# Up projections of a two-part transformer kernel: gate and value columns interleaved in the weight pieces, so that each stationary tile is every second column

## The chip, the cores and the metric

The kernel runs on one core of one Trainium2 chip. The time is device microseconds of one execution. The kernel before took 2694.57 us, the median of 3 runs (2691.31, 2694.57 and 2696.43 us).

## The reference, cut to what matters

The input is one sequence of 512 tokens with 1024 features in float32. A first block (an indexer-sparse attention beside a latent attention) is followed by four layers, each with a mixer (differential, stick-breaking, sliding-window, differential) and a feed-forward part; a norm closes it. The change touches the feed-forward part of the four layers alone. What that part computes is, as its kernel uses it:

```python
g = rmsnorm(h, ffn_norm) @ w_up          # w_up is 1024 x 5504: 2752 gate columns, then 2752 value columns
g = causal_conv_width_3(g) + conv_b      # per column
hidden = silu(g[:, :2752]) * g[:, 2752:]
h = h + hidden @ w_down
```

Every gate column is multiplied with the value column of the same number, so a gate tile and its value tile of 128 columns are produced one after the other.

## The kernel before, in words

Activations lie transposed: features on the 128 partitions, the 512 tokens along the free dimension, so 1024 features are KT = 8 tiles. Weights come from the host as "pieces" of 128 x 2048 floats (1 MB), cut and ordered there (`weight_pieces`, `piece`). Three slots of SBUF hold three pieces. SP loads a piece into `raw` when the piece three before it has been used (L1252). ACT copies it to `whi` in the reduced-precision form of float32 (L1270), and GpSimd writes `wlo` = `raw` - `whi` in four parts over the same memory (L1219). The activations are split in the same way into `xh` and `xl`.

A product of full precision is then three matmuls, issued by `three_passes` (L481): `whi` x `xh`, `whi` x `xl`, `wlo` x `xh`, all into one PSUM bank. In a feature piece the weights are the stationary operand (128 x 128) and the activations the moving one (128 x 512). A matmul record comes with a weight-load record (LDWEIGHTS); in the rows "ring<-xh,wlo" is a matmul with `wlo` stationary and `xh` moving.

An up stage (`up`, L1134) handles 22 pieces. Each of the first 21 holds, for every k of the 8 feature tiles, 256 columns: 128 gate columns, then the 128 value columns that belong to them. `first_piece` (piece 0, in an order of its own because its activations are only just being split, with the norm's sum of squares between) and `feature_piece` (pieces 1 to 20) both call `feature_group(slot, half, k, ...)`, which takes columns k*256 + half*128 to k*256 + half*128 + 127: half 0 is the gate, half 1 the value. That is 21 x 2 x 8 x 3 = 1008 passes a layer, 4032 in the kernel. Piece 21 holds only 64 gate and 64 value columns side by side; it is one stationary tile of 128 contiguous columns and 24 passes a layer.

The results go round four PSUM banks (`ring`). VectorE multiplies each with the norm's factor (L2405, into `u`), ScalarE makes the first tap of the convolution (L1695) and the silu (L1698), VectorE the other taps (L2391), the product (L2415), and the split of the hidden activations for the down projection (L2417, L2419). The engines run through fixed programs and meet at counting semaphores; each queue is in the order that the Python loops issue. `feature_group` is also called by `index_q`, by the latent stages, by `project` and by `early_out`, for pieces whose layout is not touched.

Of the kernel before, what the change touches and what calls it, by code (L numbers as in the profile page):

```python
# [14 lines left out]
P = 128  # L15
S = 512
D = 1024
KT = D // P
# [456 lines left out]
def three_passes(pe, out, w_hi, w_lo, x_hi, x_lo, first, last, weights_stationary=True):  # L475

    passes = [(w_hi, x_hi), (w_hi, x_lo), (w_lo, x_hi)]
    if not weights_stationary:
        passes = [(x_hi, w_hi), (x_hi, w_lo), (x_lo, w_hi)]
    for n, (stationary, moving) in enumerate(passes):  # L480
        ins = pe.matmul(out, stationary, moving, start=first and n == 0, stop=last and n == 2)  # L481
    return ins


def tensor_program(pe, m, st, plan):
    by_vector = vector_pieces(st)

    def wait_piece(b, k):

        p = b.at("piece", k)  # L490
        if p in by_vector:
            pe.wait_ge(m["own_lo"], by_vector.index(p) + 1)
        else:
            pe.wait_ge(m["lo_done"], p - sum(v < p for v in by_vector))

    def wait_unit_free(b, k):

        if b.at("unit_taken", k) >= 4:
            pe.wait_ge(m["unit_taken"], b.at("unit_taken", k) - 3)

    def feature_group(slot, half, k, x, out):

        w = slice(k * 256 + half * P, k * 256 + (half + 1) * P)
        return three_passes(pe, out, m.whi[slot][:, w], m.wlo[slot][:, w], *x, k == 0, k == KT - 1)

    def first_piece(b, nb, signal):


        wait_piece(b, 0)
        slot = b.slot("piece", 0, SLOTS)  # L510
        out = [m.ring[b.slot("unit_ready", half, 4)][:] for half in range(2)]
        for half in range(2):
            wait_unit_free(b, half)
            for k in range(KT - 1):
                if half == 0:
                    pe.wait_ge(m["xl_ready"], b.at("xl_ready", k + 1 - KT))
                feature_group(slot, half, k, X[k], out[half])
                yield
        pe.wait_ge(m["xl_ready"], b.at("xl_ready", 0))
        for half in range(2):  # L520
            feature_group(slot, half, KT - 1, X[KT - 1], out[half]).then_inc(m[signal], 1)
            if half == 0:
                square_sum(nb)
            yield

    def feature_piece(b, j, xs):

        wait_piece(b, j)
        slot = b.slot("piece", j, SLOTS)
        for half in range(2):  # L530
            wait_unit_free(b, 2 * j + half)
            out = m.ring[b.slot("unit_ready", 2 * j + half, 4)][:]
            for k in range(KT):
                ins = feature_group(slot, half, k, xs[k], out)
            ins.then_inc(m["unit_ready"], 1)

    def token_group(slot, t, k, out):
# [18 lines left out]
    X = [(m.xh[:, k, :], m.xl[:, k, :]) for k in range(KT)]  # L556

    def square_sum(nb):

        pe.wait_ge(m["sq_added"], nb.at("sq_added", 0))  # L560
        pe.matmul(m.out[:], m.ones[:], m.var[:], start=True, stop=True).then_inc(m["sq_summed"], 1)
# [570 lines left out]
        work.finish()  # L1132

    def up(b, nb):  # L1134
        for _ in first_piece(b, nb, "unit_ready"):
            pass
        for j in range(1, LAST):
            feature_piece(b, j, X)
        wait_piece(b, LAST)
        slot, unit = b.slot("piece", LAST, SLOTS), 2 * LAST  # L1140
        wait_unit_free(b, unit + 1)
        for k in range(KT):
            w = slice(k * P, (k + 1) * P)
            ins = three_passes(pe, m.ring[b.slot("unit_ready", unit, 4)][:], m.whi[slot][:, w], m.wlo[slot][:, w],
                               *X[k], k == 0, k == KT - 1)
        ins.then_inc(m["unit_ready"], 2)

    for name in plan:
        b = st[name]
# [1380 lines left out]
def piece(w):  # L2530

    k, n = w.shape
    kt = -(-k // P)
    a = np.zeros((kt * P, n), w.dtype)
    a[:k] = w
    a = a.reshape(kt, P, n).transpose(1, 0, 2).reshape(P, kt * n)
    if kt * n == 2048:
        return a
    full = np.zeros((P, 2048), w.dtype)
    full[:, :kt * n] = a  # L2540
    return full


def column_pieces(w):
    return [piece(w[:, c:c + 256]) for c in range(0, w.shape[1], 256)]


def mixer_pieces(mixer, w):
    if mixer == "window":
        q, k, v = (column_pieces(part) for part in np.split(w, [D, D + 256], axis=1))  # L2550
        return [k[0], q[0], v[0], *q[1:]]
    q, k, v = np.split(w, 3, axis=1)
    out = []
    for t in range(TILES):
        out.append(piece(np.concatenate([q[:, P * t:P * t + P], k[:, P * t:P * t + P]], axis=1)))
        if t % 2:
            out += column_pieces(v[:, 256 * (t // 2):256 * (t // 2) + 256])
    return out


def weight_pieces(x):
    w = x["w_in"][0]
    q_a, k_a, v_a, g_a, q_i, k_i, w_i, c_q, c_kv, k_r, g_b = np.split(
        w, np.cumsum([512, 512, 512, 512, 512, 64, 8, Q_LORA, KV_LORA, B_ROPE]), axis=1)
    rest = np.concatenate([c_q[:, 256:], k_i, w_i, k_r, np.zeros((D, 24), w.dtype)], axis=1)
    out = []
    for part in (rest, q_i, c_q[:, :256]):
        out += column_pieces(part)
    out += [piece(x["w_uq"][0][:, c:c + 384]) for c in (0, 384)]
    out += column_pieces(c_kv)  # L2570
    out.append(piece(x["w_ukv"][0]))
    for part in (k_a, q_a, v_a):
        out += [piece(part[:512]), piece(part[512:])]
    for part in (g_b, g_a):
        out += column_pieces(part)
    out += column_pieces(np.concatenate([x["w_out"][0][512:], x["w_out"][0][:512]]))
    for l in range(N_LAYERS):
        name = {"diff": "da", "stick": "sb", "window": "sw"}[MIXER[l]]
        out += mixer_pieces(MIXER[l], x[f"{name}_w_qkv_2"][MIXER[:l].count(MIXER[l])])
        out += column_pieces(x["w_o_2"][l])  # L2580
        up, f = x["ffn_w_up_2"][l], x["ffn_w_up_2"].shape[2] // 2
        for t in range(F_TILES):
            n = min(P, f - t * P)
            out.append(piece(np.concatenate([up[:, t * P:t * P + n], up[:, f + t * P:f + t * P + n]], axis=1)))
        down = x["ffn_w_down_2"][l]
        for c in range(0, D, 256):
            k = 0
            for nk in DOWN_K:
                rows = np.zeros((nk * P, 256), w.dtype)
                got = down[k * P:(k + nk) * P, c:c + 256]  # L2590
                rows[:got.shape[0]] = got
                if got.shape[0] < nk * P:
                    rows[-HALF:] = got[-HALF:]
                out.append(piece(rows))
                k += nk
    return np.stack(out)
# [73 lines left out]
```

## Time and profile before

| what | value |
|---|---|
| median of 3 runs | 2694.57 us (2691.31 to 2696.43) |
| span of the profiled execution | 2693.6 us |
| TensorE matmul records | 2653.5 us busy (99%), 12935 |
| TensorE weight-load records | 2126.5 us busy (79%), 12935 |
| VectorE, ScalarE, GpSimd busy | 1460.7, 1122.8, 1167.0 us (54, 42, 43%) |
| mean granted TensorE clock | 0.997 |
| DMA | 253.44 MB, mean 94 GB/s |

The profiled execution is given by its span, from the first to the last instruction; what lies around the span (launch and end) has no row. The span is 1.0 us under the median and 2.8 us under the highest of the runs. How to read the rows: PE is TensorE's matmuls, PEld its weight loads, which run beside them; DVE is VectorE, ACT ScalarE, POOL GpSimd, SP the queue that issues most DMAs. Matmul records overlap one another, since they contain the time through the array, so that the distance from one start to the next tells the pace and the length of a record does not.

### The profile page before, as it was taken

The page shows a single profiled execution, that of the slowest core. Times are in us where ns is not written, and L with a number is a line of the kernel's source. Part 1 is how long each engine was busy: PE and PEld are TensorE (multiplying, and loading weights), DVE is VectorE, ACT ScalarE, POOL GpSimd, SP SyncE. Part 2 cuts the span into 40 slices and gives each one's busy share as a digit, 9 for nine tenths or more (in the row PEclk, how much of TensorE's full clock was granted, in tenths as well). Part 3 has the DMA queues.
Part 4 walks back from the last instruction along what each step waited for, and adds up shares of the span by engine and source line. Part 5 has one row for each costly group of instructions (what it writes and reads, how often), then busy time and mean ns, then how long its engine had stood idle before and what let it go on. Part 6 is the DMA issues. An engine that isn't in the chain of part 4 may idle for free.

```text
span 2693.6 us, 32187 instructions
## 1 busy us (share of the span) xinstructions
PE 2653.5 (99%) x12935; PEld 2126.5 (79%) x12935; DVE 1460.7 (54%) x2615; ACT 1122.8 (42%) x1521; POOL 1167.0 (43%) x880
## 2 busy tenths in 40 slices
PE   8999999999999999999999999999999999999998
PEld 7787677778888877778888876888888777888887
DVE  5888556657554145657554145575522565575522
ACT  4544544444333236653333236443333344443332
POOL 3454443335445532335445541354455332454453
PEclk9999999999999999999999999999999999999999
DMA  4224032222223221112223331222233222222232
GB/s 164 79 94 172 1 133 86 70 73 96 106 96 110 104 88 63 63 65 98 104 94 110 109 110 48 79 94 98 106 109 110 94 87 71 94 94 94 94 122 81
DMA packets 46597, 253.44 MB, mean 94 GB/s; under 512 B 4528, under 2 KB 11200, under 8 KB 18928
## 3 DMA queue, kind: packets, MB, share of 16 engines
q1 hardware_dynamic: 35376, 231.92, 24.3%
q10 hardware_dynamic: 11072, 19.47, 2.2%
q8 instruction: 102, 1.67, 0.2%
q14 instruction: 47, 0.39, 0.0%
HBM read 249.21 MB, written 10.55 MB: 96 GB/s over the span
## 4 chain that ended last, share of the span: by engine, by line
PE 92%; DVE 4%; ACT 2%; POOL 1%; issue 1%; DMA 0%; SPq 0%; DVEq 0%; ACTq 0%
PE ring L481 79%; PE ring L978 3%; PE turn L983 2%; PE turn L481 1%; PE out L1022 1%; POOL wlo L1219 1%; PE ring L776 1%; PE ring L645 1%; PE out L792 1%; DVE sp L2238 1%; PE out L1028 0%; DVE e L2206 0%; PE out L1110 0%; ACT whi L1270 0%; DVE z L2241 0%
## 5 line engine op out<-in xcount | busy, mean ns | idle before, releaser
L1219 POOL TENSOR_TENSOR wlo<-raw,whi 128x512 fp32r<-128x512 f32 x840 | 1121.8, 1367 | 1456.9 <-ACT whi L1270 1456.8
L481 PE MATMUL ring<-xh,whi 128*128 128x512 f32 x1888 | 753.4, 399 | 9.3 <-DVE xl L1753 8.4
L481 PE MATMUL ring<-xh,wlo 128*128 128x512 f32 x1888 | 736.6, 390 | 0.0
L481 PE MATMUL ring<-xl,whi 128*128 128x512 f32 x1888 | 736.5, 390 | 0.0
L1270 ACT ACTIVATE whi<-raw 128x2048 fp32r<-128x2048 f32 x215 | 411.3, 1914 | 437.1 <-DMA raw<-in_pieces 421.8
L481 PEld LDWEIGHTS ring<-xh,whi 128*128 128x128 f32 x1888 | 354.9, 188 | 114.9 <-issue 41.1
L481 PEld LDWEIGHTS ring<-xh,wlo 128*128 128x128 f32 x1888 | 354.9, 188 | 75.3
L481 PEld LDWEIGHTS ring<-xl,whi 128*128 128x128 f32 x1888 | 355.2, 188 | 72.3 <-issue 3.4
L2391 DVE SCALAR_TENSOR_TENSOR taps<-u,conv,taps 128x511 f32<-128x511 f32 (+1 forms) x344 | 295.7, 905 | 17.3 <-ACT taps L1695 14.8
L2405 DVE TENSOR_TENSOR u<-ring,r 128x512 f32<-128x512 f32 x168 | 114.4, 687 | 299.7 <-PE ring L481 299.7
L481 PE MATMUL ring<-hh,whi 128*128 128x512 f32 (+1 forms) x693 | 265.3, 383 | 0.0
L481 PE MATMUL ring<-hl,whi 128*128 128x512 f32 (+1 forms) x693 | 265.1, 383 | 0.0
L481 PE MATMUL ring<-hh,wlo 128*128 128x512 f32 (+1 forms) x693 | 265.1, 383 | 0.0
L1695 ACT ACTIVATE taps<-u,conv 128x512 f32<-128x512 f32 x172 | 137.9, 809 | 304.5 <-DVE u L2405 304.5
L2379 DVE TENSOR_TENSOR h<-ring,h 128x512 f32<-128x512 f32 x64 | 44.1, 689 | 317.8 <-PE ring L861 277.2
L481 PE MATMUL ring<-whi,xh 128*128 128x256 f32 (+1 forms) x576 | 180.9, 314 | 0.8 <-POOL wlo L1219 0.8
L481 PE MATMUL ring<-wlo,xh 128*128 128x256 f32 (+1 forms) x576 | 172.9, 300 | 0.0
L481 PE MATMUL ring<-whi,xl 128*128 128x256 f32 (+1 forms) x576 | 172.8, 300 | 0.0
L481 PEld LDWEIGHTS ring<-hh,wlo 128*128 128x128 f32 x693 | 130.2, 188 | 25.5
L481 PEld LDWEIGHTS ring<-hh,whi 128*128 128x128 f32 x693 | 130.2, 188 | 25.4
L481 PEld LDWEIGHTS ring<-hl,whi 128*128 128x128 f32 x693 | 130.2, 188 | 25.4
L1698 ACT ACTIVATE taps<-taps 128x512 f32<-128x512 f32 x88 | 55.7, 633 | 172.3 <-DVE taps L2391 172.3
(304 smaller groups left out, 3423.0 us busy)
## 6 DMA issues: line engine op xcount, KB each, us to landing
raw<-in_pieces SPq DMA_DIRECT2D x215, 1024.0 KB, 4.8
toep<-diag_store ACTq DMA_DIRECT2D x16, 512.0 KB, 3.6
diag_store<-diag_row ACTq DMA_DIRECT2D x1, 5120.0 KB, 25.6
band_store<-band_row ACTq DMA_DIRECT2D x1, 3072.0 KB, 33.1
h<-in_x SPq DMA_DIRECT2D x4, 512.0 KB, 6.3
wbias<-band_store ACTq DMA_DIRECT2D x4, 512.0 KB, 7.2
raw<-in_pieces SPq DMA_DIRECT2D x4, 256.0 KB, 6.4
result<-h SPq DMA_DIRECT2D x2, 512.0 KB, 3.0
```

The costliest lines, as they stand in the source:

```text
L481: ins = pe.matmul(out, stationary, moving, start=first and n == 0, stop=last and n == 2)
L645: ins = pe.matmul(out, x[:, tok], weights[slot][:, w], start=begins, stop=ends)
L776: pe.matmul(bank(("score", p, j, i))[:, 0:n], q[:, i * P:(i + 1) * P], k[:, 0:n], start=True, stop=True).then_inc(m["unit_ready"], 1)
L978: pe.matmul(m.ring[2 + j][:, 0:n], qs[part, i * P:(i + 1) * P], ks[part, lo:lo + n], start=True, stop=True).then_inc(m["su_ready"], 1)
L983: ins = pe.transpose(m.turn[:, to:to + P], src[:, at:at + P], m.ident[:])
L1219: ins = pool.tensor_tensor(m.wlo[slot][:, part], m.raw[slot][:, part], m.whi[slot][:, part].bitcast(F32), ALU.subtract)
L1270: act.activation(m.whi[p % SLOTS][:], m.raw[p % SLOTS][:], ACT.Copy).then_inc(m["hi_done"], 1)
L1695: act.activation(taps[g][:], m.u[g][:], ACT.Identity, scale=cols[:, 4 * g + 2:4 * g + 3], bias=cols[:, 4 * g + 3:4 * g + 4]).then_inc(m["t ...
L1698: act.activation(taps[0][0:rows, :], taps[0][0:rows, :], ACT.Silu).then_inc(m["silu"], 1)
L2379: dve.tensor_tensor(m.h[:, k, :], ring(b, k)[:], m.h[:, k, :], ALU.add).then_inc(m["unit_taken"], 1)
L2391: dve.scalar_tensor_tensor(y[:, shift:S], m.u[g][:, 0:S - shift], cols[:, tap:tap + 1], y[:, shift:S], ALU.mult, ALU.add).then_inc(m[signa ...
L2405: dve.tensor_tensor(m.u[g][:], ring(b, 2 * t + g)[:], m.r[:], ALU.mult).then_inc(m["unit_taken"], 1)
```

## The change

In pieces 0 to 20 of every up stage the host lays gate and value columns alternately: gate 0, value 0, gate 1, value 1 and so on, 256 columns for each k as before. `feature_group` gets a flag `paired`; with it the stationary tile is every second column of the 256, from column `half` on, 128 columns at a distance of 8 bytes, where it was 128 adjacent columns at a distance of 4 bytes. `first_piece` and `feature_piece` pass the flag on, and only `up` sets it. Piece 21 keeps its layout and its code.

```diff
-    def feature_group(slot, half, k, x, out):
+    def feature_group(slot, half, k, x, out, paired=False):
 
         w = slice(k * 256 + half * P, k * 256 + (half + 1) * P)
+        if paired:
+            w = slice(k * 256 + half, (k + 1) * 256, 2)
         return three_passes(pe, out, m.whi[slot][:, w], m.wlo[slot][:, w], *x, k == 0, k == KT - 1)
...
     def up(b, nb):
-        for _ in first_piece(b, nb, "unit_ready"):
+        for _ in first_piece(b, nb, "unit_ready", True):
             pass
         for j in range(1, LAST):
-            feature_piece(b, j, X)
+            feature_piece(b, j, X, True)
...
         for t in range(F_TILES):
             n = min(P, f - t * P)
-            out.append(piece(np.concatenate([up[:, t * P:t * P + n], up[:, f + t * P:f + t * P + n]], axis=1)))
+            pair = [up[:, t * P:t * P + n], up[:, f + t * P:f + t * P + n]]
+            out.append(piece(np.stack(pair, axis=2).reshape(D, 2 * n) if n == P else np.concatenate(pair, axis=1)))
```

## Rows read from the trace of the kernel before

**Rows 1.** The page: span, busy shares, TensorE clock, shares of the last-ending chain.
```profile
span 2693.6 us, 32187 instructions
...
PE 2653.5 (99%) x12935; PEld 2126.5 (79%) x12935; DVE 1460.7 (54%) x2615; ACT 1122.8 (42%) x1521; POOL 1167.0 (43%) x880
...
PEclk9999999999999999999999999999999999999999
...
PE 92%; DVE 4%; ACT 2%; POOL 1%; issue 1%; DMA 0%; SPq 0%; DVEq 0%; ACTq 0%
```

**Rows 2.** Chain in order of time, layer 2: start us, length us, what.
```profile
1746.02 6.40 POOL wlo L1219 x4
1752.42 0.04 issue
1752.47 237.61 PE ring L481 x1047
```

**Rows 3.** Four up stages by windows: busy us (and count) of each engine.
```profile
core 0: us, PE busy (x) PEld busy (x) DVE busy (x) ACT busy (x) POOL busy (x), PEclk, DMA share, GB/s
605.60:860.00 254.40, 254.18 (x1119) 209.77 (x1119) 150.97 (x227) 97.43 (x95) 123.79 (x95) 1.00 0.28 100
1210.90:1465.30 254.40, 254.17 (x1120) 209.78 (x1119) 152.01 (x227) 97.63 (x95) 123.42 (x95) 1.00 0.28 100
1730.00:1984.00 254.00, 253.78 (x1118) 209.46 (x1117) 154.85 (x227) 97.71 (x95) 126.09 (x97) 1.00 0.28 100
2329.00:2583.00 254.00, 253.79 (x1118) 209.47 (x1117) 152.35 (x228) 97.63 (x95) 123.93 (x95) 1.00 0.28 100
```

**Rows 4.** Timeline inside an up stage, matmuls and weight loads: start us, length us.
```profile
640.15 0.39 PE L481 MATMUL ring<-xh,whi 128*128 128x512 f32 x1
640.16 0.19 PEld L481 LDWEIGHTS ring<-xl,whi 128*128 128x128 f32 x1
640.38 0.39 PE L481 MATMUL ring<-xl,whi 128*128 128x512 f32 x1
640.38 0.19 PEld L481 LDWEIGHTS ring<-xh,wlo 128*128 128x128 f32 x1
```

**Rows 5.** Timeline around the only wait of TensorE in an up stage.
```profile
627.78 0.19 PEld L481 LDWEIGHTS ring<-xh,whi 128*128 128x128 f32 x1 [0.64 <-POOL wlo L1219]
627.78 0.50 PE L481 MATMUL ring<-xh,whi 128*128 128x512 f32 x1 [0.22 <-POOL wlo L1219]
627.89 0.19 PEld L481 LDWEIGHTS ring<-xl,whi 128*128 128x128 f32 x1
628.12 0.40 PE L481 MATMUL ring<-xl,whi 128*128 128x512 f32 x1
628.12 0.19 PEld L481 LDWEIGHTS ring<-xh,wlo 128*128 128x128 f32 x1
```

**Rows 6.** Timeline of a value projection of layer 0, whose moving operand has 256 columns.
```profile
540.19 0.28 PE L481 MATMUL ring<-whi,xl 128*128 128x256 f32 x1
540.31 0.28 PE L481 MATMUL ring<-whi,xh 128*128 128x256 f32 x1
...
540.19 0.19 PEld L481 LDWEIGHTS ring<-whi,xh 128*128 128x128 f32 x1
540.31 0.19 PEld L481 LDWEIGHTS ring<-wlo,xh 128*128 128x128 f32 x1
```

**Rows 7.** Groups of weight loads, whole span: busy us, mean ns of one, idle before.
```profile
L481 PEld LDWEIGHTS ring<-xh,wlo 128*128 128x128 f32 x1888 | 354.9, 188 | 75.3
L1022 PEld LDWEIGHTS out<-aT,v 128*128 128x128 f32 x128 | 23.8, 189 | 19.0 <-issue 13.1
L1110 PEld LDWEIGHTS out<-at_w,v_w 128*64 128x64 f32 x224 | 12.1, 137 | 2.9 <-issue 2.9
```

**Rows 8.** Waits inside an up stage, 628 to 860 us: total, times, longest us.
```profile
POOL wlo L1219 <- ACT whi L1270: 115.6, 23, 6.1
ACT taps L1695 <- DVE u L2405: 77.3, 23, 4.3
DVE u L2405 <- PE ring L481: 75.8, 18, 4.6
ACT taps L1698 <- DVE taps L2391: 38.6, 21, 4.2
ACT whi L1270 <- DMA raw<-in_pieces: 25.1, 18, 7.1
DVE taps L2391 <- ACT taps L1695: 3.7, 13, 1.1
PE ring L481 <- POOL wlo L1219: 0.2, 1, 0.2
```

**Rows 9.** The page: DMA issues of the weight pieces, and ACT's and GpSimd's work on them.
```profile
L1219 POOL TENSOR_TENSOR wlo<-raw,whi 128x512 fp32r<-128x512 f32 x840 | 1121.8, 1367 | 1456.9 <-ACT whi L1270 1456.8
L1270 ACT ACTIVATE whi<-raw 128x2048 fp32r<-128x2048 f32 x215 | 411.3, 1914 | 437.1 <-DMA raw<-in_pieces 421.8
...
raw<-in_pieces SPq DMA_DIRECT2D x215, 1024.0 KB, 4.8
```

More of the change, by code:

```diff
@@ L499, in wait_unit_free, with first_piece @@
             pe.wait_ge(m["unit_taken"], b.at("unit_taken", k) - 3)
-    def feature_group(slot, half, k, x, out):
+    def feature_group(slot, half, k, x, out, paired=False):
         w = slice(k * 256 + half * P, k * 256 + (half + 1) * P)
+        if paired:
+            w = slice(k * 256 + half, (k + 1) * 256, 2)
         return three_passes(pe, out, m.whi[slot][:, w], m.wlo[slot][:, w], *x, k == 0, k == KT - 1)
-    def first_piece(b, nb, signal):
+    def first_piece(b, nb, signal, paired=False):
         wait_piece(b, 0)
@@ L516, in first_piece @@
                     pe.wait_ge(m["xl_ready"], b.at("xl_ready", k + 1 - KT))
-                feature_group(slot, half, k, X[k], out[half])
+                feature_group(slot, half, k, X[k], out[half], paired)
                 yield
@@ L520, in first_piece @@
         for half in range(2):
-            feature_group(slot, half, KT - 1, X[KT - 1], out[half]).then_inc(m[signal], 1)
+            feature_group(slot, half, KT - 1, X[KT - 1], out[half], paired).then_inc(m[signal], 1)
             if half == 0:
@@ L524, in first_piece, with feature_piece @@
             yield
-    def feature_piece(b, j, xs):
+    def feature_piece(b, j, xs, paired=False):
         wait_piece(b, j)
@@ L533, in feature_piece @@
             for k in range(KT):
-                ins = feature_group(slot, half, k, xs[k], out)
+                ins = feature_group(slot, half, k, xs[k], out, paired)
             ins.then_inc(m["unit_ready"], 1)
```

## Prediction, made before the changed kernel ran

> **What bounds the kernel now.** I read the page first: TensorE's matmul records cover 99% of the span, the chain that ended last is TensorE for 92% of it, and the granted clock stands at its top digit, that is 2.4 GHz, in all 40 slices [rows 1]. Then the chain in order of time, to see what it consists of where the change acts. In layer 2 one unbroken run of 1047 passes of the helper at L481 takes 237.61 us, so one pass every 237.61/1047 = 226.9 ns; the same figure for the same count stands in the chain of the other three layers [rows 2]. The windows then show each up stage as nothing but TensorE: about 254 of 254 us, while VectorE has 151 to 155 us of work, ScalarE 98 and GpSimd 123 to 126 [rows 3]. The waits say the same from the other side: VectorE, ScalarE and GpSimd wait for what comes before them, and TensorE waits once, for 0.2 us, for GpSimd's low half of piece 2 [rows 5, 8]. So inside an up stage the time is a count of passes times the distance between their starts. The question is only whether that distance stays at 226.9 ns.
>
> The timeline shows what makes up the distance. Each weight load starts when the matmul before its own starts (640.16 beside 640.15, 640.38 beside 640.38) and its record is 0.19 us, so it ends before the next matmul begins [rows 4]. The load is thus covered by the previous matmul, and what matters is how long it really occupies its path. The record is longer than that. After the one wait, the load at 627.78 is followed by the next load at 627.89, and its own matmul, whose record is 0.50 instead of 0.39 us, is late by the same 0.11 us [rows 5]. Where the moving operand has only 256 columns, loads with records of 0.19 us start every 0.12 us and overlap one another [rows 6]. A load of 128 columns occupies the path for about 0.11 us, then, and has 0.2269 us to do it: a good half of the pass is spare.
>
> **The change part by part.**
>
> *Strided weight loads.* 4 layers x 21 pieces x 2 halves x 8 tiles x 3 passes = 4032 loads now step over 8 bytes from column to column instead of 4. Their number, columns, partitions and bytes used are as before. No row of the trace shows a load with a step, so its price has to be bounded. Every nanosecond that it adds to the distance between passes costs 4032 ns = 4.03 us. The lower bound on the cost is zero with the load's pace unchanged: the mean length of a load goes by its columns, 137 ns for 64 and 189 for 128, 0.81 ns a column [rows 7]. The next bound is a load whose pace goes by the stretch of memory it walks, 1024 bytes instead of 512: 2 x 0.11 = 0.22 us, under 0.2269, so still hidden; taken at the coarse end of the rounding, 0.23 us, it would stick out by 3.1 ns, 4032 x 3.1 ns = 12.5 us. The upper bound is a load that is no more covered at all and adds its 0.11 us to every pass, as after the wait [rows 5]: 4032 x 0.11 = 444 us. For a gain the bound is the part of a pass that isn't streaming: 256 more moving columns take 226.9 - 120 = 107 ns [rows 2, 6], so 512 take 214 and 13 ns are left; if the load made them and a step removed them, 4032 x 13 ns = 52 us would go. I see no reason why a step should.
>
> I take zero. The row it is nearest to is TensorE's other read: the moving operand walks 512 x 4 = 2048 bytes a partition in each 226.9 ns, 9.0 bytes a ns, at full pace [rows 2, 4]. A stepped load walks 1024 bytes, and if it spread them over the pass it would need only 4.5 bytes a ns; at the old 0.11 us it needs 9.3, which is what the other read does already.
>
> A rule of the Trainium skill stands against this. "Advanced Engine Details and Errata", section Memory Cachelines, says that SBUF is read in lines of 16 bytes, that accesses that stay in a line run at full pace while a different line at each access is penalised, and that two hits on a line are needed to absorb the latency; for PSUM, whose lines it gives as 8 bytes, it says that any non-contiguous pattern slows matmuls significantly. By its SBUF half a step of 8 bytes still hits each line twice and the sum stays at zero; by its PSUM half, if the load followed it, the load would double and be the second bound above. No row of the trace before tells the two apart.
>
> *The first load after a pause.* There the load is not covered [rows 5]. That happens once at the wait of each layer; if the load doubled, each would cost 0.11 us, 4 x 0.11 = 0.4 us in all. At an unchanged pace it is nothing. No other load in the stage is first after a pause.
>
> *The pieces and their path.* The host reorders columns inside a piece. The DMA still moves 1024 KB in one issue for each of the 215 pieces, ScalarE's copy is still 128 x 2048 in 1914 ns and GpSimd's four subtractions still 128 x 512 in 1367 ns [rows 9]: they read and write the whole piece in order. Cost nothing, with no cover needed. The stationary tile holds the same numbers in the same columns, so PSUM, the norm factor, the convolution's coefficients and the rest of VectorE's and ScalarE's work see the same operands. Piece 21, the mixers and the down stages use contiguous columns as before. No wait, no issue and no semaphore is added or moved, and no queue is passed.
>
> *Sum.* 2693.6 + 0 = 2693.6 us of span. The median of the runs is 1.0 us above this span; I give 2694.6 us. A measurement of this kernel can tell about 0.2% from no change, that is 5.4 us; the cost at which the change would be seen is therefore 1.3 ns a pass.
>
> **The rivals.**
>
> *The load doubles but stays in its cover.* For it: more memory is walked for each load. Against: the pace of the moving read. The load records would grow from 188 by the 104 ns that 128 columns at 0.81 take, to about 292 ns, and the distance would be 227 to 230 ns: 2694.6 to 2707 us. Chance 0.10, of which 0.06 on the side that cannot be measured.
>
> *The load outlasts the matmul (slower).* Place: the load path of the 4032 passes. It decides from an occupation of 226.9 ns on, 2.06 times the present 0.11; from there the distance is the load's own. At three times it is 0.33 us: (330 - 226.9) x 4032 = 416 us, 3110 us. The same comes out of a stepped load that isn't taken ahead of the running matmul (444 us, 3139 us). For it: the load would be the only operand of TensorE in this kernel that is not read contiguously, and nothing in the trace shows that path with a step. Against: it would need more than the doubling that the memory walked can explain. Chance 0.08.
>
> *A shorter pass (faster).* 52 us at most, 2642 us. Nothing speaks for it but the bound. Chance 0.02.
>
> *The change doesn't do what it says.* A load of a stepped tile could be issued as several loads. Then the count of weight loads would leave 12935; its time would go by whether the pieces fit the 0.2269 us, so it shares the two cases above rather than having a price of its own.
>
> **How the numbers follow.** The forecast, no visible change, has 0.80. Its own range is the spread of the runs, 2691 to 2696, widened to 2687 to 2701 for another set of three. The doubled load reaches to 2707. Together these hold 0.90; I set the range to 2687 to 2709 and leave out the load that outlasts the matmul and the shorter pass. Within 0.2%: 0.80 + 0.06, less 0.01 for a forecast case that measures off, 0.85. Slower: 0.04 + 0.08 = 0.12. Faster: 0.02 + 0.01 = 0.03.
>
> **What the profile of the changed kernel would show.** If the step is free: weight loads in `ring<-xh,wlo` still at 188 ns, 12935 of them, the chain's run of 1047 passes still 237.6 us. If the load doubled under cover: a minimum near 188 and a maximum near 292 ns in that group, matmuls still 0.227 us apart, and the first matmul after the wait at piece 2 late by 0.22 instead of 0.11 us. If the load binds: the run of passes in the up stages longer than 237.6 us with everything else as it was, VectorE waiting longer for `ring`, and TensorE's 0.2 us wait for GpSimd gone. I would be wrong if a pass in an up stage stands more than 1.3 ns further from the next than before.

## The result, and the profile after

The changed kernel took 2720.24 us (median of 4 runs, 2718.94 to 2721.48) against 2695.5 us for the kernel before: a ratio of 1.0095, 95% interval 1.0082 to 1.0107. The 2695.5 us are the median of 4 runs, one of which took 9223.89 us; that one is not in the ratio, and the other three have a median of 2694.57 us. The changed kernel is slower by 25 us, where no change was forecast, and outside the range of 2687 to 2709. In the profiled executions the span went from 2693.6 to 2718.9 us, 25.3 us more.

The page of the kernel after, against [rows 1]:

```profile
span 2718.9 us, 32187 instructions
...
PE 2680.5 (99%) x12935; PEld 2149.0 (79%) x12935; DVE 1449.9 (53%) x2615; ACT 1122.3 (41%) x1521; POOL 1163.9 (43%) x880
```

The counts of instructions are those of before, so no load was split into several. VectorE, ScalarE and GpSimd have the same counts, and nearly the same busy times, as before. TensorE's matmul records grew by 27 us in sum, its loads by 22.5 us. The chain in order of time of the kernel after, layer 0:

```profile
599.99 15.49 PE ring L481 x67
615.47 0.86 PE out L563 x2
616.33 255.47 PE ring L481 x1098
```

Nothing but TensorE is in it any more. Before, the chain went through ScalarE's copy and GpSimd's 6.40 us [rows 2] up to the wait at piece 2; both have dropped out of it, since TensorE comes to piece 2 later. What is left of the wait is short:

```profile
628.13 0.20 PEld L481 LDWEIGHTS ring<-xh,whi 128*128 128x128 f32 x1 [0.35 <-POOL wlo L1221]
628.13 0.51 PE L481 MATMUL ring<-xh,whi 128*128 128x512 f32 x1
628.25 0.20 PEld L481 LDWEIGHTS ring<-xl,whi 128*128 128x128 f32 x1
```

The first load still waits 0.35 us for GpSimd where it waited 0.64 [rows 5], and no matmul is put down as waiting any more. So the loss is not a new wait. These lines show something else: the load at 628.13 has a step and is not covered, and the next load starts 0.12 us after it, where it was 0.11 [rows 5]. In the starts of the trace that is 117 ns against 108. The load with a step did not double.

The windows of the same 200 us inside the up stage of layer 0, matmuls of `three_passes` alone (length, busy us and count, granted clock as a share of 2.4 GHz, DMA share, GB/s), first of the kernel before, then of the kernel after:

```profile
640.00:840.00 200.00, 200.00 (x884) 1.00 0.28 100
```

```profile
640.00:840.00 200.00, 200.00 (x859) 1.00 0.27 95
```

The clock is full in both and TensorE is never idle, but 25 passes fewer fit in. Groups of one tile, min/median/max of a record in ns, in 40 us of that stage, before and after:

```profile
L481 PE MATMUL ring<-xl,whi x60: 389/389/389, 639.7 to 679.8; 128*128 128x512 f32 x60
L481 PEld LDWEIGHTS ring<-xh,whi x59: 187/188/188, 639.9 to 679.4; 128*128 128x128 f32 x59
```

```profile
L481 PE MATMUL ring<-xl,whi x58: 394/394/394, 639.7 to 679.6; 128*128 128x512 f32 x58
L481 PEld LDWEIGHTS ring<-xh,whi x58: 193/193/193, 639.9 to 679.8; 128*128 128x128 f32 x58
```

A load's record is 5 ns longer, a matmul's too, and not one of them is an exception, although ScalarE, GpSimd, VectorE and the DMAs start and stop their work many times in those 40 us. A loss to another engine should come and go with that engine's work. The distance from start to start, in the timeline of the kernel after over 40 passes:

```profile
649.70 0.39 PE L481 MATMUL ring<-xh,wlo 128*128 128x512 f32 x1
...
659.04 0.39 PE L481 MATMUL ring<-xh,whi 128*128 128x512 f32 x1
```

9.34 / 40 = 233.5 ns; over a whole unit the trace gives 233.3, against 226.7 before. 4032 passes x 6.66 ns = 26.9 us. The shorter wait for GpSimd (0.3 us less in each layer, 1.2 us) comes off, and each up stage is 6.3 us longer, 25.3 us for four: the whole difference.

In all that follows "distance" is the mean distance from one matmul's start to the next within a unit of 24 passes, without its first three, read from the starts in the timeline of layer 0; "plain" is a tile of adjacent columns, "stepped" one of every second column. A "unit" is the gate or the value product of one piece, and a piece has one of each.

### The profile page after: what moved, and what is told of

Same layout as the page of the kernel before. It is cut to its first block, busy times and chain, and to the rows that moved or that the text cites. A ratio compares the mean times of both kernels' runs of the same rounds, so it can differ in the third digit from the quotient of the medians.

```text
span 2718.9 us, 32187 instructions
## 1 busy us (share of the span) xinstructions
PE 2680.5 (99%) x12935; PEld 2149.0 (79%) x12935; DVE 1449.9 (53%) x2615; ACT 1122.3 (41%) x1521; POOL 1163.9 (43%) x880
## 4 chain that ended last, share of the span: by engine, by line
PE 95%; DVE 3%; ACT 1%; issue 1%; POOL 0%; DMA 0%; SPq 0%; DVEq 0%; ACTq 0%
PE ring L481 81%; PE ring L980 3%; PE turn L985 2%; PE turn L481 1%; PE out L1024 1%; PE ring L647 1%; PE ring L778 1%; PE out L794 1%; DVE sp L2240 1%; PE out L1030 0%; DVE e L2208 0%; PE out L1112 0%; DVE z L2243 0%; PE out L1072 0%; PE out L563 0%
## 5 line engine op out<-in xcount | busy, mean ns | idle before, releaser
L481 PEld LDWEIGHTS ring<-xh,whi 128*128 128x128 f32 x1888 | 362.1, 192 | 115.5 <-issue 41.2
L481 PEld LDWEIGHTS ring<-xh,wlo 128*128 128x128 f32 x1888 | 361.9, 192 | 76.8
L481 PEld LDWEIGHTS ring<-xl,whi 128*128 128x128 f32 x1888 | 362.3, 192 | 73.9 <-issue 3.3
L2393 DVE SCALAR_TENSOR_TENSOR taps<-u,conv,taps 128x511 f32<-128x511 f32 (+1 forms) x344 | 282.8, 866 | 24.3 <-ACT taps L1697 23.6
L481 PEld LDWEIGHTS ring<-whi,xh 128*128 128x128 f32 x576 | 110.4, 192 | 21.1 <-issue 13.9
```

The source lines that it names most:

```text
L2393: dve.scalar_tensor_tensor(y[:, shift:S], m.u[g][:, 0:S - shift], cols[:, tap:tap + 1], y[:, shift:S], ALU.mult, ALU.add).then_inc(m[signa ...
```

## The experiments

The diffs are against the changed kernel and are cut; `...` marks a cut. The host's side is cut throughout: it goes back to the layout before in `step3`, `offset1`, `offset4`, `narrow_plain`, `w384_plain`, `offsets` and `moving_step`, and is laid out to fit in `step4` and `step8`. Most of these kernels compute a product of other columns or tokens than the reference's, as their expectations say; they are for their times. From `step3` on, each ran once, beside one run of the kernel before (2693.86 to 2696.37 us).

### Whose cost is it: the step, or the new order of the data?

`host_only` keeps the host's new order and takes plain tiles. `value_only` steps in half of the loads.

```diff
# host_only
-        if paired:
-            w = slice(k * 256 + half, (k + 1) * 256, 2)
# value_only
-        if paired:
+        if paired and half == 1:
             w = slice(k * 256 + half, (k + 1) * 256, 2)
```

> The pieces keep the new order of columns from the host, but every stationary tile is again 128 adjacent columns (so a tile holds half of a gate tile and half of its value tile, and the hidden features are not the reference's). If the step of the load is the cause: the distance between passes in an up stage goes back from 233.3 to 226.7-226.9 ns and the time to 2694 to 2696 us, ratio to the kernel before 1.000. If the new order of the data is the cause (other values in the same places, the DMA or the split): it stays at 233 ns and 2720 us.

> Only the value tile (half 1) is read with the step, the gate tile (half 0) as 128 adjacent columns; the gate product is therefore of other columns than the reference's. 2016 stepped loads instead of 4032. If each stepped load costs its own matmul 6.5 ns: the 24 passes of a gate unit 226.7 ns apart, those of a value unit 233.3 ns, and half the loss, 2695.5 + 12.6 = 2708 us. If the odd start column (4 bytes off) makes the cost rather than the step: nearly the whole loss stays, 2720 us. If the stage loses for another reason (contention with the engines that write the pieces): no clean split by unit.

Measured: `host_only` 2694.62 us, ratio 0.9999 (0.9990 to 1.0009). `value_only` 2707.38 us, ratio 1.0047 (1.0032 to 1.0062), half the loss, with 226.7 ns in the gate units and 233.3 in the value units that alternate with them. The cost goes with the addressing of the unit's own loads, and it begins and ends with the unit. Data, DMA and the split are out.

### More step

`step4` and `step8` interleave two and four feature tiles in the same manner; `step3` takes every third column.

```diff
# step4: tile = every 4th of 512 columns; step8: every 8th of 1024
-            w = slice(k * 256 + half, (k + 1) * 256, 2)
+            w = slice(512 * (k // 2) + 2 * (k % 2) + half, 512 * (k // 2 + 1), 4)
...
# step3
+            w = slice(min(k, 6) * 256 + half, min(k, 6) * 256 + 384, 3)
```

> Two feature tiles are interleaved, so that a stationary tile is every fourth column (16 bytes) of 512. If the cost goes by how many different 16-byte stretches a load touches (32 adjacent, 64 with step 2, 128 with step 4): three times the extra, +20 ns a pass, 247 ns, 2695.5 + 4032 x 0.020 = 2776 us. If any step costs the same: 233.3 ns and 2720 us. If the load's pace by bytes walked decides and was hidden at step 2: 4 x 0.11 = 0.44 us a pass, 3550 us.

> Four feature tiles interleaved, every eighth column (32 bytes) of 1024. If the cost goes by 16-byte stretches touched: 128 of them as with step 4, so the same time as step4. If it goes by the memory walked: seven times the extra of step 2, +46.7 ns a pass, 273 ns, 2883 us. If any step costs the same: 2720 us.

> Every third column (12 bytes) of 384 (the last feature tile takes the one before it; the product is of other columns than the reference's). If a load keeps its pace as long as two of its columns share a 16-byte stretch on average at least, and halves it below that: 1.33 columns a stretch here, so a load record between 193 (step 2) and 310 ns (step 4), near 260, and a distance of 233 to 235 ns. If the halving comes only when every column has a stretch of its own: 193 ns. Time near 2721 to 2725 us either way.

Measured: `step4` 2725.05 us, ratio 1.0112 (1.0095 to 1.0129); `step8` 2767.3 us, 1.0269 (1.0254 to 1.0284); `step3` 2726.97 us. The distances are 235.0, 244.3 and 235.8 ns. None of the theories had that order: step 3 costs a little more than step 4, step 4 hardly more than step 2, and step 8 much more than step 4. The load records, `step3`, `step4`, `step8`:

```profile
L481 PEld LDWEIGHTS ring<-xl,whi x57: 252/252/253, 640.0 to 679.6; 128*128 128x128 f32 x57
```

```profile
L481 PEld LDWEIGHTS ring<-xh,whi x57: 308/310/311, 639.9 to 679.4; 128*128 128x128 f32 x57
```

```profile
L481 PEld LDWEIGHTS ring<-xl,whi x55: 324/331/337, 639.9 to 679.6; 128*128 128x128 f32 x55
```

Here the load really becomes slower: 188 ns with adjacent columns, 193 with step 2, 252 with step 3, 310 with step 4, and no more than 331 with step 8. How long a load really occupies its path shows at the wait at piece 2. There `step4` has

```profile
625.83 0.31 PEld L481 LDWEIGHTS ring<-xh,whi 128*128 128x128 f32 x1 [0.15 <-POOL wlo L1221]
625.84 0.62 PE L481 MATMUL ring<-xh,whi 128*128 128x512 f32 x1
...
626.04 0.33 PEld L481 LDWEIGHTS ring<-xl,whi 128*128 128x128 f32 x1
```

The next load follows after 108 ns with adjacent columns, 117 with step 2, 165 with step 3 and 211 with step 4, by the starts in the traces (`step8` has no such wait). At step 4 a load is thus twice as long, and the pass is still only 235.0 ns: the cover held. So two things are to be told apart, the load's length, which is hidden up to step 4, and a few ns a pass that are not. Whether the load of `step8` still fits its pass of 244.3 ns is open.

### Is the loss in the load's own time?

`offset1` and `offset4` use plain tiles, of the layout before, that begin one and four columns further on, all but the last value tile of a piece.

```diff
         w = slice(k * 256 + half * P, k * 256 + (half + 1) * P)
-        if paired:
-            w = slice(k * 256 + half, (k + 1) * 256, 2)
+        if paired and (k, half) != (KT - 1, 1):
+            w = slice(w.start + 1, w.stop + 1)        # offset4: 4
...
```

> Adjacent columns again, but every tile but the last begins one column (4 bytes) further on, so that its first and last 16-byte stretch are cut; the product is of shifted columns. If the 6.6 ns of step 2 come from an access that is not whole 16-byte stretches from a 16-byte boundary: 233.3 ns and 2720 us here too. If they come from the step: 226.7 ns and 2695 us.

> As offset1, with every tile but the last four columns (16 bytes) further on. If it is the cut 16-byte stretches at a tile's ends that cost offset1 its 5.8 ns a pass: none here, 226.7 ns and 2695 us. If any start other than a multiple of 512 bytes costs: 232 ns and 2714 us.

Measured: 2714.42 and 2712.61 us. There is no step in either, and most of the loss is there: 232.4 and 232.7 ns in `offset1`, 233.2 to 233.4 in three of the four layers of `offset4`. The tile's records in `offset1`, 40 us of layer 0:

```profile
L481 PE MATMUL ring<-xl,whi x58: 388/392/399, 639.8 to 679.6; 128*128 128x512 f32 x58
L481 PEld LDWEIGHTS ring<-xh,whi x58: 187/187/188, 640.1 to 679.8; 128*128 128x128 f32 x58
```

The loads are as fast as ever (187 ns, and 109 ns to the next one after the wait), and only the matmuls are late. That ends the theory that a pass loses because its load takes longer. 16-byte stretches that are cut at a tile's ends aren't it either, since `offset4`, shifted by 16 bytes, has none.

`offset4` holds another thing. Windows of 200 us in the up stages of layer 0 and layer 2, same program, same instructions:

```profile
640.00:840.00 200.00, 200.00 (x860) 1.00 0.27 94
...
1770.00:1970.00 200.00, 200.00 (x883) 1.00 0.27 95
```

From piece 3 on, layer 2 ran at 226.7 ns, the other three layers at 233.3. The same addresses have two steady rhythms. The trace shows where they part: layers 0 and 2 have the same distances, ns for ns, up to the wait before piece 2, where the distance is 332 ns in layer 0 and 327 in layer 2. After it the pattern of distances stands in another order, and at the last tile of piece 2, the one without a shift, layer 2 goes over to 226.7 ns and keeps it. The 5 ns in that wait are the first difference that the trace shows, so a small delay seems to decide the pace of the rest of the stage; no other run tests it.

### Narrower moving operands

In pieces 1 to 20, `narrow_plain` and `narrow_step` do the 512 tokens in two halves of 256, and `w384_plain` and `w384_step` compute 384 of the 512. In each pair only the loads differ.

```diff
# narrow_*
-            for k in range(KT):
-                ins = feature_group(slot, half, k, xs[k], out, paired)
+            for tok in TOKENS if paired else (slice(0, S),):
+                for k in range(KT):
+                    ins = feature_group(slot, half, k, [v[:, tok] for v in xs[k]], out[:, tok], paired)
...
# w384_*
+            n = 384 if paired else S
...
+                ins = feature_group(slot, half, k, [v[:, 0:n] for v in xs[k]], out[:, 0:n], paired)
```

> In pieces 1 to 20 of each up stage the moving operand is cut into two halves of 256 tokens, adjacent columns, pieces as before the change: 7680 passes in place of 3840. From the projections of the kernel before, 120 ns a pass: 240 instead of 226.7 ns for 512 tokens, 3840 x 13.3 = 51 us more than 2695.5, 2747 us, if GpSimd's split of the pieces keeps up (a piece needs 11.5 us of TensorE and 5.4 us of GpSimd).

> The same cut with the stepped loads of the change, against narrow_plain. If a stepped load adds a fixed time that no matmul covers: 126.7 ns a pass, 7680 x 6.67 = 51 us more than narrow_plain, plus 192 x 6.67 = 1 us for piece 0. If a stepped load really takes twice its time and was hidden: at 120 ns it isn't any more, and a pass is 213 ns or more, over 700 us more. If it only slows the moving operand's read while both run: the load runs beside the whole of a narrow pass, so again about 6.67 ns a pass.

> Pieces 1 to 20 of each up stage compute 384 of the 512 tokens, adjacent columns; the rest of a bank is left from before, so the hidden features of tokens 384 to 511 are not the reference's. Stream 160.0 ns and the 13.3 ns that every plain pass has shown beyond its stream: 173.3 ns a pass, 3840 x 53.3 = 205 us less, 2490 us.

> As w384_plain with the stepped loads. At 512 moving columns the step cost 6.67 ns a pass and at 256 nothing. If the loss is a rounding of the pass to a grid of 6.67 ns (all mean distances so far are multiples of that over a short repeating pattern): 173.3 or 180.0 ns or a pattern between. If the loss grows with the part of a pass in which no load runs: half of it, 176.7 ns. If the loss is there as soon as the load ends before the stream: 180 ns.

Measured: `narrow_plain` 2741.82 us, `narrow_step` 2741.87 us: with 256 moving columns 7680 stepped loads cost nothing that can be seen. Their tiles, plain and stepped:

```profile
L481 PE MATMUL ring<-xh,whi x112: 283/283/283, 639.8 to 679.8; 128*128 128x256 f32 x112
L481 PEld LDWEIGHTS ring<-xl,whi x112: 192/192/192, 639.8 to 679.8; 128*128 128x128 f32 x112
```

```profile
L481 PE MATMUL ring<-xl,whi x112: 281/284/288, 639.7 to 679.7; 128*128 128x256 f32 x112
L481 PEld LDWEIGHTS ring<-xh,whi x112: 194/196/198, 639.8 to 679.8; 128*128 128x128 f32 x112
```

The distance is 120.0 ns in both; in the stepped kernel it goes round in fours (123, 123, 115, 119 ns, their sum 480). A load that occupied its path for more than 120 ns would show here; the 117 ns of a stepped one just fit. A stepped load that adds an uncovered time of its own would show too, and it doesn't. At 384 columns the same: `w384_plain` 2576.21 us and `w384_step` 2574.73 us, 173.3 ns a pass in both where TensorE had not just waited, with load records of 188 and 194 ns. The 2490 us expected were missed because the convolution then bounds the stage: a piece takes VectorE and ScalarE 9.1 us one behind the other and TensorE 8.3 us. The stretches in which TensorE ran were enough to read the distance.

The distances 120.0, 173.3 and 226.7 ns at 256, 384 and 512 columns lie on a line: 128 columns more take 53.3 ns, 2.4 columns a ns, and 13.3 ns are left over. That line is the last column of the next table.

`widths` changes the moving operand from piece to piece, gate plain and value stepped.

> Value tiles stepped, gate tiles adjacent; in pieces 1 to 20 of each up stage the moving operand has 512, 504, 496, ... 400, then 512, 510, 508, 506, 512 columns, so part of the tokens is left out, and the gate product is of other columns. If the loss is a rounding to a grid of 6.67 ns (16 moving columns): the distances of both kinds of unit are in stairs of 16 columns, and the stepped ones sit a stair higher at some widths and level with the plain ones at others (384: level). If the loss is there from some width on: plain goes by (columns/2.4 + 13.3) ns throughout, and stepped parts from it at one width between 384 and 512.

| moving columns | plain, ns | stepped, ns | stream (columns/2.4) + 13.3 |
|---|---|---|---|
| 512 | 226.7 | 233.3 | 226.7 |
| 510 | 226.7 | 233.3 | 225.8 |
| 508 | 227.4 | 226.7 | 225.0 |
| 506 | 226.7 | 226.7 | 224.2 |
| 504 | 227.6 | 226.7 | 223.3 |
| 496 | 223.3 | 225.3 | 220.0 |
| 488 | 225.9 | 220.0 | 216.7 |
| 480 | 216.7 | 216.7 | 213.3 |
| 472 | 213.3 | 213.3 | 210.0 |
| 464 | 208.9 | 211.7 | 206.7 |
| 456 | 208.2 | 204.4 | 203.3 |
| 448 | 206.4 | 203.3 | 200.0 |
| 440 | 200.0 | 199.8 | 196.7 |
| 432 | 195.2 | 193.3 | 193.3 |
| 424 | 190.0 | 193.4 | 190.0 |
| 416 | 188.3 | 186.7 | 186.7 |
| 408 | 185.0 | 186.7 | 183.3 |
| 400 | 180.7 | 180.0 | 180.0 |

Neither theory held. Stepped is worse at 512, 496 and 424, better at 504, 488 and 448, level at 480 and 472; at 508 and 506 the loss of the stepped tile is gone. It isn't the step that costs as such: which of the two is better changes from width to width, and the plain 512 is a lucky case, at the floor of stream + 13.3 ns. No unit of an up stage in these runs went below that floor by more than 0.2 ns.

### Position in memory

`offsets` has 512 moving columns and plain tiles that begin further on from piece to piece.

```diff
+SHIFTS = (0, 1, 2, 3, 4, 6, 8, 12, 16, 20, 24, 32, 48, 64, 80, 96, 112, 128, 120, 0)
...
         if paired:
+            shift = min(SHIFTS[paired - 1], 2048 - P - w.start)      # paired: number of the piece
+            w = slice(w.start + shift, w.stop + shift)
```

> All tiles adjacent and 512 moving columns; in pieces 1 to 20 every tile begins 0, 1, 2, 3, 4, 6, 8, 12, 16, 20, 24, 32, 48, 64, 80, 96, 112, 128, 120, 0 columns further on (the last tiles of a piece less, so as to stay in it), so the product is of shifted columns. If two reads of TensorE get in each other's way by their position in blocks of 64 bytes (the moving operand passes 64 bytes in 6.67 ns): a shift of 16, 32, 48, 64 ... columns is free, 226.7 ns, and those between cost 5 to 7 ns. If only a start at a multiple of 512 bytes is free: 0 and 128 alone. If a tile's start is of no account and offset1 and offset4 lost for their last tile, which isn't shifted: shifts of 1 to 128 all lose.

Distance by shift of the gate tiles, in columns of 4 bytes:

| shift | 0 | 1 | 2 | 3 | 4 | 6 | 8 | 12 | 16 | 20 | 24 | 32 | 48 | 64 | 80 | 96 | 112 | 128 |
|---|---|---|---|---|---|---|---|---|---|---|---|---|---|---|---|---|---|---|
| ns | 226.7 | 232.6 | 230.7 | 230.0 | 233.4 | 231.1 | 233.3 | 233.3 | 233.3 | 232.0 | 234.2 | 232.6 | 228.8 | 226.7 | 233.3 | 232.6 | 228.8 | 226.7 |

The timeline at shifts 16 and 64, the fourth and the last pass of a gate unit, 20 passes apart (4.66/20 = 233, 4.53/20 = 226.5 ns):

```profile
707.24 0.39 PE L482 MATMUL ring<-xh,whi 128*128 128x512 f32 x1
...
711.90 0.39 PE L482 MATMUL ring<-xh,wlo 128*128 128x512 f32 x1
...
762.93 0.39 PE L482 MATMUL ring<-xh,whi 128*128 128x512 f32 x1
...
767.46 0.39 PE L482 MATMUL ring<-xh,wlo 128*128 128x512 f32 x1
```

The row repeats: 16, 32, 48 and 64 columns give 233.3, 232.6, 228.8, 226.7, and so do 80, 96, 112 and 128. The period is 64 columns, 256 bytes. The expected blocks of 64 bytes were wrong by a factor of four. Counted from the start of the activations, the tiles of the kernel before start at a multiple of 256 bytes, the one start in this table with a free pass; only layer 2 of `offset4` had one at another start.

`moving_offset` leaves the weights in place and starts the moving operand (448 columns) further on.

```diff
...
-            for k in range(KT):
-                ins = feature_group(slot, half, k, xs[k], out, paired)
+            n, at = (448, SHIFTS[j - 1]) if paired else (S, 0)
+            for k in range(KT):
+                ins = feature_group(slot, half, k, [v[:, at:at + n] for v in xs[k]], out[:, 0:n], paired)
```

> Value tiles stepped, gate tiles adjacent at their places; 448 moving columns that begin 0, 1, 2, 3, 4, 6, 8, 12, 16, 20, 24, 28, 32, 40, 48, 56, 60, 64, 62, 0 columns into their tile, so tokens are left out or shifted. If the position of the two reads to each other decides: gate units lose at some starts (200 ns at 0, up to 206.7 ns), the stepped ones at others, with free starts for the stepped ones too. If only the stationary operand's addresses count: 200 ns for the gate units at every start, and one value for the value units.

Plain / stepped at a start of 0 columns 202.7/203.3 ns, at 3 columns 200.0/206.7, at 16 columns 200.2/203.3, at 24 columns 205.3/202.3, at 48 columns 202.3/200.4, at 62 columns 208.3/206.8. So the moving operand's address counts as well, and for other starts the stepped load is the better one. The plain unit at 0 has 202.7 here and 206.4 in `widths`, at the same width and the same addresses modulo 256 bytes: as in `offset4`, more than one rhythm.

`pads_a` and `pads_b` then move the three weight slots in memory, gate plain and value stepped, 512 columns.

```diff
+PADS = (0, 64, 128)                                   # pads_b: (32, 96, 192)
...
+        for i in range(SLOTS):
+            self.top += (self.place["xh"] + PADS[i] - self.top) % 256
+            self.raw.append(self.keep(f"raw{i}", [P, 2048]))
+            self.whi.append(self.keep(f"whi{i}", [P, 2048], F32R))
```

> Weight slots 0, 1 and 2 (raw, whi) begin 0, 64 and 128 bytes off a multiple of 256 bytes, counted from the activations; value tiles stepped, gate tiles adjacent, 512 moving columns; the gate product is of other columns. If the position of the loads to the moving operand decides: adjacent tiles 226.7, 233.3 and 232.6 ns in pieces of the slots 0, 1 and 2, as the shifts of 0, 16 and 32 columns in offsets, in the w_o and down stages too; stepped ones 233.3 in slot 0 and, after the 48 columns of moving_offset (a load 64 bytes ahead, modulo 256), near 227 in slot 1. If the step alone decides: 233.3 ns for stepped tiles in every slot.

> As pads_a with 32, 96 and 192 bytes. If position decides: adjacent tiles 233, 232 and 228.8 ns (offsets: shifts of 8, 24, 48 columns; 20 gave 232.1), the stepped ones different from slot to slot between 226.7 and 235. If the step alone decides: 233.3 ns for stepped tiles in every slot.

| slot begins at, bytes modulo 256, counted from `xh` | 0 | 32 | 64 | 96 | 128 | 192 |
|---|---|---|---|---|---|---|
| plain, ns | 226.7 | 233.0 | 233.3 | 234.2 | 232.5 | 228.8 |
| stepped, ns | 233.3 | 231.8 | 230.0 | 230.0 | 231.5 | 233.3 |

Stepped tiles in `pads_a` at 0 and at 64 bytes, 20 passes apart, 4.67/20 = 233.5 and 4.60/20 = 230 ns:

```profile
694.12 0.39 PE L485 MATMUL ring<-xh,whi 128*128 128x512 f32 x1
...
698.79 0.39 PE L485 MATMUL ring<-xh,wlo 128*128 128x512 f32 x1
...
705.31 0.39 PE L485 MATMUL ring<-xh,whi 128*128 128x512 f32 x1
...
709.91 0.40 PE L485 MATMUL ring<-xh,wlo 128*128 128x512 f32 x1
```

The plain tiles repeat the table of `offsets` at 8, 16, 24, 32 and 48 columns to within 0.3 ns, in another kernel and by another way to the same address. The stepped ones change with the slot, so the position counts for them too; but the 227 ns expected at 64 bytes were 230.0, half the loss, and none of six positions was free. Whole kernels: 2729.43 and 2733.58 us, more than the 2707.38 of `value_only`; the slots are shared with every other stage, and their plain tiles then start off a multiple of 256 bytes as well. The same run of passes in the down stage of layer 0, before and in `pads_a`:

```profile
869.70 25.16 PE ring L481 x111
```

```profile
879.14 25.56 PE ring L485 x111
```

That is 3.6 ns a pass more. Of the 34.0 us by which the span of `pads_a` is longer, the up stages hold 18.3 and the w_o and down stages 10.6; most of the rest lies in other products that use the slots.

`columns` changes the size of the tile, gate plain and value stepped, 512 moving columns.

```diff
...
+            n = COLUMNS[paired - 1]
+            w = slice(k * 256 + half, k * 256 + 2 * n, 2) if half else slice(k * 256, k * 256 + n)
+            out = out[0:n, :]
```

> 512 moving columns; in pieces 1 to 20 a tile has 128, 126, 124, 120, 112, 104, 96, 80, 64, 48, 32, 128, 96, 64, 32, 128, 96, 64, 32, 128 columns, adjacent for gate units, stepped for value units; the rest of the features is left out. If the loss is in how a stepped load begins: 233.3 against 226.7 ns at every number of columns. If it comes from how long the load reads beside the stream: it shrinks with the columns and is gone at 32. If it hangs on where the load's reads fall in a block (it reads the tile from one end): it comes and goes with the number of columns, for adjacent tiles too.

Plain / stepped at 128 columns 226.7/233.3 ns, 126: 233.4/231.1, 124: 226.7/233.3, 112: 229.1/226.7, 96: 230.0/230.9, 64: 230.2/231.2, 48: 235.0/230.3, 32: 231.7/233.2. A load of a quarter of the length doesn't help, and most tiles lose 2 to 8 ns, plain or stepped, while a plain one of 124 columns and a stepped one of 112 lose nothing; only the third theory is left of the three.

### The moving operand with a step

`moving_step` has plain stationary tiles; its moving operand takes every second column of two feature tiles.

```diff
+                x = xs[k] if not paired else [
+                    v[:, min(k, KT - 2):min(k, KT - 2) + 2, :].rearrange("p k s -> p (k s)")[:, ::2] for v in (m.xh, m.xl)]
...
```

> Stationary tiles adjacent as before the change; in pieces 1 to 20 the moving operand takes every second column of two feature tiles (8 bytes apart), so the product is of other activations. If a read of TensorE keeps its pace while two of its columns share a 16-byte stretch, and the 6.6 ns of the change belong to the load: 226.7 ns. If a step shifts any read's start in the same way: 233.3 ns, 2721 us. If the moving read, which goes twice as fast as the load, can't keep its pace with a step: 2 x 213 ns, over 800 us more.

Measured: 3564.17 us. The timeline:

```profile
650.03 0.63 PE L481 MATMUL ring<-xl,whi 128*128 128x512 f32 x1
650.49 0.63 PE L481 MATMUL ring<-xh,wlo 128*128 128x512 f32 x1
650.94 0.63 PE L481 MATMUL ring<-xh,whi 128*128 128x512 f32 x1
651.39 0.64 PE L481 MATMUL ring<-xl,whi 128*128 128x512 f32 x1
```

The distance is 453 ns, twice. So the moving read, at 2.4 columns a ns, halves its pace with 8 bytes a column, while the load, whose 128 columns take 108 ns, hardly loses any (117 ns). An estimate from these numbers puts both on one scale. Count the 16-byte stretches that a read touches: the moving read goes through 128 of them in 226.7 ns and, stepped, through 256 in 453 ns; after the wait the loads with steps 2, 3 and 4 go through 64, 96 and 128 of them in 117, 165 and 211 ns. That is 1.65 to 1.83 ns for each stretch in all five, 8.8 to 9.7 bytes walked a ns. Adjacent columns take the moving read to that pace already; the load gets there at step 2. By the bytes walked a load of `step8` would take twice as long as one of `step4`, by the stretches as long: its records are 331 ns against 310, so the stretches fit better, and not fully. It is a pattern in these numbers, not a shown mechanism.

## Why the prediction was wrong

**What held.** The bound was read rightly: an up stage is a count of passes times their distance, and the whole loss is that product, less the shorter wait. The other parts were costed rightly at nothing: `host_only` is at 0.9999, the work of DMA, ScalarE and GpSimd is unchanged, and no load was split. The spare time under a matmul was read rightly as well: the doubled load that stood among the bounds was made in `step4` (211 ns instead of 108), and its pass is 235.0 ns, 8.3 ns from the plain one rather than 103. The argument from the moving read held for the pace: the load nearly kept it at step 2 (a record of 193 ns, not 292; 117 ns to the next load). It held without a margin, though. The 9.0 bytes a ns of the moving read are about as much as it can walk (`moving_step`), and a load at step 3 or 4 was slower.

**The step that failed** is the cost of the strided weight loads, the one from "A load of 128 columns occupies the path for about 0.11 us" to "I take zero". It made the load's length the only thing that a step could change, and the cover the only test. The row that spoke against it stood in the text: of a pass's 226.7 ns only 213.3 are stream, and the 13 ns beyond were used as a bound on a gain alone. They are the part that no cover hides, and they could grow as well as go. They grew to 20.0 ns: the term put at zero measured 6.66 ns a pass, 26.9 us, with the load still covered. No row before the change told that they would grow. But a bound on the side of the loss as wide as the one on the side of the gain would have been 4032 x 13.3 ns = 54 us, 2748 us as an estimate of the upper end in place of 2707, and the measured 2720 lies inside.

**The rivals.** The doubled load under its cover named a distance of 227 to 230 ns by another mechanism; the load outlasting the matmul would have needed 330 ns; the shorter pass did not come. None was it, and the four chances had no place for a covered load with a longer pass. No load was split, the count is still 12935. The profile shows the signs that the prediction gave for a load that binds (the run of passes longer, TensorE's 0.2 us wait gone, VectorE waiting longer for `ring`: 82.1 instead of 75.8 us from 628 to 860 us), and yet the load does not bind: these signs belong to any longer pass. Only the last sentence, wrong if a pass is more than 1.3 ns longer, told rightly what to look at.

**The rule on 16-byte lines** from the Trainium skill, "Advanced Engine Details and Errata", section Memory Cachelines, describes the load's own pace well: two columns on a line 193 ns, fewer than that 252 and 310 ns. For the moving read it does not hold, since a step of 8 bytes has two columns on a line too and the pass doubles (`moving_step`); the measurement decides. It said nothing of the few ns that the pass lost, and the doubling that the prediction drew from its PSUM half did not come (117 ns against 108).

**What is shown and what is not.** Shown: the loss of this change comes from the addresses of its 4032 loads (`host_only`, `value_only`). A loss of that size needs no step (`offsets`) and no longer load (`offset1`), and the distance stays constant through all the other engines' work. It goes by the load's address modulo 256 bytes (`offsets`, `pads_a`, `pads_b`), by the moving operand's start (`moving_offset`), by its width (`widths`, `narrow_step`, `w384_step`) and by the tile's size (`columns`), and the same addresses can have two rhythms (`offset4`). That would fit two reads of TensorE, load and moving operand, that meet in memory and settle into a repeating pattern whose length follows from their positions to each other. This reading is argued, not shown: no run separates a meeting in memory from another dependence on both addresses, and which addresses meet stays open. The nearest to a test, the forecast of 227 ns for a stepped tile at 64 bytes, got the direction and half the size.

## What to carry to other kernels

Don't take a weight load for free because it ends well under the matmul: with 512 moving columns a pass here was stream + 13.3 ns where the tile was adjacent and started at a multiple of 256 bytes from the activations, and mostly 2 to 8 ns more elsewhere; with 384 and 256 columns the step cost nothing. Where a kernel is one long run of passes, a few ns a pass are a per cent of its time. So keep the columns of a stationary tile adjacent, start tiles at a multiple of 256 bytes from the moving operand, and let the host lay the weights out so. Give the moving operand no step: 8 bytes from column to column doubled the pass.

## What the runs showed that was not expected

- The record of a load of 128 columns by its step: 188, 193, 252, 310 and 331 ns at 1, 2, 3, 4 and 8 columns. The time to the next load where nothing covers it: 108, 117, 165 and 211 ns at 1, 2, 3 and 4.
- A stepped moving operand: 453 against 226.7 ns.
- Adjacent tiles shifted by 16 columns cost as much as a step of 2 (233.3 ns); the pattern repeats every 256 bytes.
- One program with two rhythms: 233.3 ns a pass in three layers and 226.7 in the other (`offset4`); the first difference between them in the trace is 5 ns in a wait.
- Several distances are whole multiples of 6.67 ns: 34 of them for the plain pass of 512, 35 for the stepped one, 18 for 256 columns, 26 for 384. Others fall between, 34.5 at 230.0 ns and 35.25 at 235.0.
